# Padding behind the slots of split weights and behind the k-tiles of the normalized stream

## The reference, cut to what matters

```python
def first_block(x, c, ...):
    shift, scale, gate = jnp.split(silu(c) @ w_ada + b_ada, 3, axis=-1)
    h = rms_norm(x) * (1.0 + scale) + shift
    xr, gr, qc, kvc, kr, ga = jnp.split(h @ w_in, ...)
    y_rnn = rg_lru_branch(xr, ...) * silu(gr)
    y_att = mla_branch(qc, kvc, kr, ...) * silu(ga)
    return x + gate * (jnp.concatenate([y_rnn, y_att], -1) @ w_out)

def second_block(x, ...):                 # two layers
    h = h + _diff_attention(_rmsnorm(h, g), a_w_qkv, ..., a_w_o)      # layer 0
    h = h + _conv_ffn(_rmsnorm(h, g), ffn_w_up[0], ..., ffn_w_down[0])
    kv = _rmsnorm(h, kv_norm_g) @ b_w_kv
    h = h + _stick_breaking(_rmsnorm(h, g), b_w_q, k, v, b_w_o)       # layer 1
    h = h + _conv_ffn(_rmsnorm(h, g), ffn_w_up[1], ..., ffn_w_down[1])

def _conv_ffn(xn, w_up, conv_w, conv_b, w_down):
    up = xn @ w_up                        # 2048 -> 2 x 5632
    u, g = up[..., :D_FF], up[..., D_FF:]
    g = causal depthwise conv of width 3 over g, + conv_b
    return (silu(g) * u) @ w_down         # 5632 -> 2048
```

## Time and profile before

| what | before |
|---|---|
| median of 3 runs | 2834.27 us (2834.07 to 2836.99) |
| profiled execution, its own time | 2835.27 us |
| its span, first to last instruction | 2833.5 us |
| mean granted TensorE clock | 0.993 |
| PE busy | 2766.6 us (98%) |
| PEld busy | 2388.8 us (84%) |
| DVE busy | 1981.3 us (70%) |
| ACT busy | 1189.0 us (42%) |
| matmuls on line 639 | 13,056 |
| DMA | 527.14 MB, mean 186 GB/s |

### The profile page before, as it was taken

The page is one execution under the profiler, slowest core; times in us unless marked ns, Lnnn a source line. Parts: engine busy times, 40 slices in busy tenths (PEclk is TensorE's granted clock), DMA queues, the critical chain, the costliest instruction groups (busy, mean ns, idle before and its releaser), DMA issues.

```text
span 2833.5 us, 44014 instructions
## 1 busy us (share of the span) xinstructions
PE 2766.6 (98%) x15284; PEld 2388.8 (84%) x15284; DVE 1981.3 (70%) x2609; ACT 1189.0 (42%) x1517; POOL 5.7 (0%) x12
## 2 busy tenths in 40 slices
PE   6899999999999999999999999999999999999999
PEld 4787888888878888888888888888888888888888
DVE  6555477676767777756777666688777775677765
ACT  1102454444444444444444543355444444444443
POOL 0000000000000000000000000000000000000000
PEclk9999999999999999999999999999999999999999
DMA  9886655544545666666666566654466666666664
GB/s 295 291 265 196 208 188 181 175 139 144 160 129 170 179 187 192 183 192 189 183 188 191 183 193 190 181 163 126 152 182 185 190 184 193 187 187 185 191 199 144
DMA packets 704736, 527.14 MB, mean 186 GB/s; under 512 B 31693, under 2 KB 694031, under 8 KB 704399
## 3 DMA queue, kind: packets, MB, share of 16 engines
q1 hardware_dynamic: 701728, 523.67, 61.1%
q10 hardware_dynamic: 2927, 2.39, 0.3%
HBM read 523.87 MB, written 2.10 MB: 186 GB/s over the span
## 4 chain that ended last, share of the span: by engine, by line
PE 89%; DVE 5%; issue 2%; ACT 2%; DMA 1%; ACTq 0%; DVEq 0%; SPq 0%
PE acc L639 76%; PE acc L719 2%; PE acc L707 2%; PE acc L908 2%; PE turned L719 1%; DVE wr L1646 1%; PE sums L719 1%; DVE pro_ada L1721 1%; DMA aring<-in_w_ada 1%; PE sums L647 1%; PE mixed L829 1%; PE sums L1023 1%; PE mixed L1028 0%; ACT wr L1205 0%; ACTq L1236 0%
## 5 line engine op out<-in xcount | busy, mean ns | idle before, releaser
L639 PE MATMUL acc<-xs,wr 128*128 128x512 f32 (+1 forms) x7680 | 1365.2, 339 | 1.1 <-DVE wr L1646 1.1
L639 PEld LDWEIGHTS acc<-xs,wr 128*128 128x128 f32 x7680 | 1176.8, 188 | 177.2 <-issue 7.2
L1646 DVE TENSOR_TENSOR wr<-raw,wr 128x1024 fp32r<-128x1024 f32 x832 | 1001.8, 1222 | 363.6 <-ACT wr L1205 351.7
L1205 ACT ACTIVATE wr<-raw 128x1024 fp32r<-128x1024 f32 x832 | 869.7, 1057 | 818.6 <-PE acc L639 812.1
L639 PE MATMUL acc<-ys,wr 128*128 128x512 f32 (+1 forms) x4352 | 769.5, 338 | 6.7 <-DVE ys L1680 6.5
L639 PEld LDWEIGHTS acc<-ys,wr 128*128 128x128 f32 x4352 | 668.4, 188 | 103.1 <-DVE ys L1680 6.4
L639 PE MATMUL acc<-wr,xs 128*128 128x512 f32 (+1 forms) x1024 | 190.1, 344 | 0.0
L639 PEld LDWEIGHTS acc<-wr,xs 128*128 128x128 f32 x1024 | 158.2, 188 | 27.1 <-issue 4.3
L1539 ACT ACTIVATE ffn_cv<-ffn_cv 128x256 f32<-128x256 f32 x88 | 36.8, 419 | 245.8 <-DVE ffn_cv L2220 245.8
L1657 DVE TENSOR_REDUCE ffn_ug<-acc 128x512 f32<-128x1024 f32 x88 | 107.8, 1225 | 42.5 <-PE acc L639 42.5
L1721 DVE SCALAR_TENSOR_TENSOR pro_ada<-aring,small,pro_ada 128x512 f32<-128x512 f32 (+1 forms) x112 | 92.5, 826 | 30.1 <-DMA aring<-in_w_ada 23.5
(11 more groups left out here) (306 smaller groups left out, 1530.4 us busy)
## 6 DMA issues: line engine op xcount, KB each, us to landing
raw<-in_ffn_w_up SPq DMA_DIRECT2D x704, 256.0 KB
raw<-in_ffn_w_down SPq DMA_DIRECT2D x160, 512.0 KB
raw<-in_a_w_qkv SPq DMA_DIRECT2D x96, 512.0 KB
raw<-in_b_w_kv SPq DMA_DIRECT2D x64, 512.0 KB
aring<-in_w_ada SPq DMA_DIRECT2D x96, 256.0 KB, 6.8
w<-in_w_in SPq DMA_DIRECT2D x48, 512.0 KB
raw<-in_w_ada SPq DMA_DIRECT2D x32, 512.0 KB, 5.7
raw<-in_w_out SPq DMA_DIRECT2D x32, 512.0 KB
```

What stands on the lines that cost most here:

```text
L639: mm = pe.matmul(*ops, start=first and ops is wide, stop=last and ops is wide)
L1205: f(wr[:, s, :, 0:256], raw[:, s, :].rearrange("p (k n) -> p k n", k=UK), ACT.Copy)\
L1646: tt(wr[:, s, :, 256:512], raw[:, s, :].rearrange("p (k n) -> p k n", k=UK), wr[:, s, :, 0:256], ALU.subtract).then_inc(T.unit_split[s].se ...
```

## The change

A constant `PAD = 8` (floats, so 32 bytes). Each of the four slots of `wr` becomes 8 floats longer, and each of the 16 k-tiles of `xs` too. The padding is never read or written. All uses name the part without the padding. The buffers that lie over `wr` and `xs` start where those start and have no padding of their own; `ys` has none.

```diff
+PAD = 8
...
-        wr = sb("wr", [RING, UK, 512], F32R)
+        wr = sb("wr", [RING, UK * 512 + PAD], F32R)
+
+        def wr_tiles(slot):
+
+            return wr[:, slot, 0:UK * 512].rearrange("p (k n) -> p k n", k=UK)
+
...
-        xs = sb("xs", [KT, 2 * TOK], F32R)
-        xs_at = nc.sbuf_base - KT * 2 * TOK * 4
+        xs = sb("xs", [KT, 2 * TOK + PAD], F32R)
+        xs_at = nc.sbuf_base - KT * (2 * TOK + PAD) * 4
...
-                        w, x, first, last = wr[:, s, k - k0, :], right(k), k == 0, k == blocks - 1
+                        w, x, first, last = wr_tiles(s)[:, k - k0, :], right(k), k == 0, k == blocks - 1
...
-                    pair(lambda k: xs[:, k, :], before=None if live else normed, after=in_q)
+                    pair(lambda k: xs[:, k, 0:2 * TOK], before=None if live else normed, after=in_q)
...
-                    f(wr[:, s, :, 0:256], raw[:, s, :].rearrange("p (k n) -> p k n", k=UK), ACT.Copy)\
+                    f(wr_tiles(s)[:, :, 0:256], raw[:, s, :].rearrange("p (k n) -> p k n", k=UK), ACT.Copy)\
...
-                    tt(wr[:, s, :, 256:512], raw[:, s, :].rearrange("p (k n) -> p k n", k=UK), wr[:, s, :, 0:256],
+                    tt(wr_tiles(s)[:, :, 256:512], raw[:, s, :].rearrange("p (k n) -> p k n", k=UK), wr_tiles(s)[:, :, 0:256],
```

More of the change, by code:

```diff
@@ L1071, in in_v @@
                             diff_turn(kA, 1)
-                    pair(lambda k: xs[:, k, :], before=None if live else normed, after=in_q)
-                    pair(lambda k: xs[:, k, :], after=in_k)
-                    pair(lambda k: xs[:, k, :], after=in_v, tokens_out=True)
+                    pair(lambda k: xs[:, k, 0:2 * TOK], before=None if live else normed, after=in_q)
+                    pair(lambda k: xs[:, k, 0:2 * TOK], after=in_k)
+                    pair(lambda k: xs[:, k, 0:2 * TOK], after=in_v, tokens_out=True)
             two_heads(True)
@@ L1104, in ffn @@
                     if g == 0:
-                        pair(lambda k: xs[:, k, :], before=normed_by, after=lambda n: stream_sums() if n == 1 else None)
-                        pair(lambda k: xs[:, k, :])
+                        pair(lambda k: xs[:, k, 0:2 * TOK], before=normed_by, after=lambda n: stream_sums() if n == 1 else None)
+                        pair(lambda k: xs[:, k, 0:2 * TOK])
                     with T.turns(pe, GROUP // 2 - (g == 0), **splits(2 * UK), acc_read=2):
                         for e in range(2):
-                            pair(lambda k: xs[:, k, :])
+                            pair(lambda k: xs[:, k, 0:2 * TOK])
                     residual_product(GROUP, stored=g == 1 and last, tiles=1)
@@ L1128, in _ @@
                     for e in range(2):
-                        pair(lambda k: xs[:, k, :], tokens_out=part == 1)
+                        pair(lambda k: xs[:, k, 0:2 * TOK], tokens_out=part == 1)
             for e in range(2):
-                pair(lambda k: xs[:, k, :], tokens_out=True)
+                pair(lambda k: xs[:, k, 0:2 * TOK], tokens_out=True)
             def stick_scores():
@@ L1168, in after @@
                             stick_sums(n - 2)
-                    pair(lambda k: xs[:, k, :], before=normed if first and e == 0 else None, after=after)
+                    pair(lambda k: xs[:, k, 0:2 * TOK], before=normed if first and e == 0 else None, after=after)
             two_query_pairs(True)
```

## The result

The changed kernel takes **2843.75 us** (2842.95 to 2844.47, 6 runs) against 2834.17 us of the kernel before beside it: a ratio of 1.0032, 95% interval 1.002 to 1.0045. It is slower by 9.6 us, which is more than the likeliest case of the forecast (no difference beyond 5.7 us) allows. The profiled execution has a span of 2842.1 us, 8.6 us more than before.

What follows compares the result with a forecast made beforehand. The prediction took PE's matmul rate on line L639 to bound the kernel. All four parts of the change summed to 0 (0 + 0 + 0 + 0), giving 2834.3 us, the median of the runs shown, with range 2826 to 2846.

Steps and rivals of the forecast that it cites:

- likeliest case: Whole kernel: no difference beyond 5.7 us, 2828.6 to 2839.9 us, chance 0.73.
- What bounds the kernel: Line L639 on PE: the rate of taking matmuls sets the time, 349.2 ns a pair, 2280 us, 80% of the span.
- Step (3): Buffers behind `wr` move by 128 bytes, those behind `xs` by 512 more; claimed effect nothing.
- The test for collisions: PE's two reads in L639: collisions would show uneven matmul counts by stretch; counts were 631 and 632, so gain 0.
- the reading side of (1) and (2): PE reading moved `wr` slots and `xs` tiles: bounds 4.0 ns a pair loss, 25.5 ns a pair gain; taken as 0.
- The prediction's last sentence: Wrong if a tile's address matters to PE at a grain the trace can't show; counts cover only steps of 512 bytes.
- rival B: L639: PE's two reads collide at fixed starts, padding makes it faster; 2730 us, or 2824 in part; chance 0.12.
- Step (1) and (2), writing side: ACT and DVE writing moved slots and tiles: at most 2 ns per write, 1.7 us, hidden by waits; taken as 0.
- Rival A: Moving read of `xs` in L639, odd tiles: starting 32 bytes off a 64-byte boundary costs 7.7 us, 2842.0 us; chance 0.15.
- 25.5 ns a pair: L639: unaccounted time, 349.2 less 323.7 ns reckoned from full fp32 matmuls; 166 us in all, the most padding could return.
- Rival C: `ys` tiles and tiles within a `wr` slot unpadded: in 2176 of 6528 pairs only slot bytes act, capping both rivals; no chance given.

Runs made afterwards that it cites:

- the version that is 50 us faster: Against the kernel before: each slot of `wr` holds four high tiles, 64 unused bytes, four low tiles, padded to 8448 bytes; 2784.61 us, ratio 0.982.
- the maps: Not the computation: PE alone multiplies two buffers at varied distances, first one distance, then two; 46 segments in 560 us, then 89 segments; 340.0 ns at best.

## Why the prediction was wrong in its likeliest case, step by step

**What bounds the kernel** was right: PE's rate on line 639. In the long stages no other engine came on the path, up to the version that is 50 us faster.

**Step (3), "nothing", is the step that failed.** A shift of `xs` and `ys` by 128 bytes against `wr` costs 15 us (shift only), one by 96 bytes wins 17. My reason was that `ys` and `xs` "lie at very different distances from `wr` and give the same 174.6 ns". They do not lie at different distances where it counts: both are 64 bytes on, within 256. The shift by 128 makes that 192, and a pair takes 353.0 ns instead of 348.9. The padding inside the buffers then softens the loss: on `xs` the rate is 353.0 with the shift alone, 350.3 with the padded slots added, 351.0 with the padded tiles as well, and 349.5 with padded tiles and no shift.

**The test for collisions failed for the same reason.** I read the even counts of the earlier trace rows as a sign of no collision, and so put the reading side of (1) and (2) at 0. The four places of the weights within a tile, 0, 1024, 512 and 1536 bytes, are all multiples of 256, the tiles all have a pitch of 2048, and both streams sat at the same distance; every matmul of those stretches was at the same distance, so the rate could not but be even. The one stretch that was not at that distance, the swapped one, was the one that differed, and I explained it by its roles. The prediction's last sentence names this hole, but a chance of 0.12 for rival B and of 0.15 for slower did not pay for it.

**Step (1) and (2), writing side**: right, within 1 ns in the medians.

**Rival A** has 7.7 us and the truth is 9.6, so the nearness is chance, for the mechanism is refuted: padding `xs` alone costs nothing measurable, and with all tiles moved by 96 bytes, 32 within 64, the kernel is faster. **Rival B** had the right place, the two reads of PE, and the wrong sign. It took 25.5 ns a pair as what padding could give back. Of these, 8.9 go away at the best placement found (348.9 to 340.0), and the other 16.3 (340.0 less the 323.7 that I had reckoned) are in every layout that was tried; whether they have to do with the two reads is not shown. And padding by 32 bytes does not remove the dependence, it deals the distances out, while the kernel before sat at one place with 348.9. That the swapped stage won, from 353.0 to 349.4, has the same root, since it sat at one of the slow distances; but the same eight distances in other orders gave it 353.6 and 354.0, so its gain does not follow from the set of distances alone. **Rival C** was right that `ys` has only the slots' bytes to act on it, and wrong that this caps the effect: it left out the shift, which acts on `ys` in full (353.0 ns alone, 351.6 with the padded slots).

**The rule from the Trainium skill** by which the change was worth nothing (page "SBUF — State Buffer", section "Who interferes with whom": PE and ACT "never wait on anyone") does not agree with these runs. With no other engine at work, the rate of PE depends on the distance of its own two reads: a wide and a short matmul take 340.0 to 353.4 ns, a spread of 13.4; the measurement decides. That writes of ACT and DVE don't slow PE's reads, as the rule has it, does agree: in the kernels with one distance throughout, the steady rates are those of the maps, where both stand still (353.3, 350.0, 346.7 and 340.0 ns), but for distance 64 with its two rates.

## What to carry to other kernels

If PE's rate sets the time, look at the addresses: what counted here is the distance between the moving tile and the weights loaded meanwhile, within 256 bytes, and an even rate over a whole kernel may only mean that all tiles have the same distance. A buffer that only moves is a change too. Don't pad to spread the distances; find a good one with a map of PE alone (one run of 1 ms tried 64 combinations) and fix it with tile pitches that are multiples of 256 bytes. The map foretold the rate of a stage when its distance was constant, and missed by 1 to 3 ns when it changed from tile to tile. Where two kinds of matmul take turns, try their two distances together, as the rates of each alone don't add up: here 64 bytes between the high and the low weights were worth 50 us of 2835, 1.8%, with the same instructions.

## What the runs showed of the hardware

- The rate of a stream of fp32r matmuls with a weight load for each depends on the distance of the two reads, with a period of 256 bytes over the 512 bytes that were tried in steps of 32; a distance of 16 gives 346.7 and one of 8 gives 353.3 ns, so what counts is finer than 32 bytes. This holds while the distance is constant. Where it changes from tile to tile, stages with the same eight distances took 349.4 to 354.0 ns.
- The fastest rates all come to the same time per moving column: 226.7 ns for 512, 113.3 for 256, 340.0 for 768 are 0.443 ns each. A record of full fp32 took 0.843 ns a column (215.8 for 256), and half of that is 0.421. What the 5% between 0.421 and 0.443 are, stays open.
- At distances 64 and 224 two steady rates of a wide and a short matmul were seen (348.9 and 353.3; 346.7 and 353.4). Alone, wide matmuls took 228.9 ns each at distance 64 and 233.3 at 832, which is 64 within 256 too, and short ones 117.8 and 113.3. So either the period is not the whole story or the entry chooses here as well; this was not told apart.
